# Delta rule: four state updates on VectorE moved from the end of a round to its middle

## What is computed

```
def step(S, inp):
    q_i, k_i, u_i, w_i, g_i, a_i = inp
    v_new = u_i - w_i @ S
    o = (q_i * exp(g_i)) @ S + a_i @ v_new
    S = S * exp(g_last) + k_dec.T @ v_new        # the state update
    return S, o
...
o = rmsnorm(o, gdn_norm_g) * silu(gate)          # needs the sum of o's squares
```

## Time and profile before

| | |
|---|---|
| median of 3 runs | 2711.78 us (2711.27 to 2712.54) |
| the profiled execution | 2711.7 us, span 2709.9 us |
| mean granted TensorE clock | 0.991 |
| busy: TensorE, weight loads, VectorE, ScalarE, GpSimd | 2604.8, 2173.4, 1664.5, 843.2, 1131.1 us |
| rounds 1 to 7 of the delta rule | roughly from 360 to 590 us |
| of 340 to 576 us: TensorE, VectorE, ScalarE, GpSimd busy | 213.64, 170.38, 73.28, 14.79 us |

### The profile page before, as it was taken

How to read it: one execution, slowest core, us unless ns; L and a number is a source line. 1 busy time by engine, 2 the same in 40 slices (tenths; PEclk the granted TensorE clock), 3 DMA queues, 4 the chain that set the end, 5 groups by cost and what they waited for, 6 DMA issues and landing times.

```text
span 2709.9 us, 33153 instructions
## 1 busy us (share of the span) xinstructions
PE 2604.8 (96%) x13218; PEld 2173.4 (80%) x13218; DVE 1664.5 (61%) x2192; ACT 843.2 (31%) x1332; POOL 1131.1 (42%) x651
## 2 busy tenths in 40 slices
PE   6999889989999999999999998999999999999998
PEld 5788778877788877888888887788888888888877
DVE  4879968766412587666674558804455465476566
ACT  4011233334223433333332436312222222243342
POOL 2433100046732546777754444663222322242364
PEclk8999999999999999999999999999999999999999
DMA  4122233235311412222245553472433342466682
GB/s 151 63 87 94 97 122 126 90 105 203 117 55 70 160 68 78 78 86 78 86 143 192 168 174 133 170 253 105 132 101 109 132 141 93 159 253 210 218 310 109
DMA packets 147381, 360.25 MB, mean 133 GB/s; under 512 B 15173, under 2 KB 51229, under 8 KB 147100
## 3 DMA queue, kind: packets, MB, share of 16 engines
q1 hardware_dynamic: 65072, 177.81, 19.6%
q10 hardware_dynamic: 82156, 180.33, 18.6%
HBM read 268.90 MB, written 89.19 MB: 132 GB/s over the span
## 4 chain that ended last, share of the span: by engine, by line
PE 84%; DVE 7%; ACT 2%; DMA 2%; POOL 2%; issue 2%; ACTq 1%; DVEq 0%; POOLq 0%
PE pp L295 31%; PE pp L2177 13%; PE pp L2230 9%; PE pp L277 8%; PE pp L493 7%; PE pp L2907 2%; PE pp L1254 2%; DMA w_raw<-in_weights 1%; POOL w_lo L3606 1%; DVE hgin_b L2713 1%; PE pp L1941 1%; PE pp L1920 1%; DVE hgin_f L2703 1%; POOL w_hi L3604 1%; PE pp L2927 1%
## 5 line engine op out<-in xcount | busy, mean ns | idle before, releaser
L3604 POOL CAST w_hi<-w_raw 128x1024 fp32r<-128x1024 f32 x184 | 222.6, 1210 | 1010.2 <-PE pp L295 678.2
L295 PE MATMUL pp<-w_hi,act_hi 128*128 128x512 f32 x1344 | 540.9, 402 | 14.1 <-POOL w_lo L3606 8.8
L295 PE MATMUL pp<-w_hi,act_lo 128*128 128x512 f32 x1344 | 527.9, 393 | 0.0
L295 PE MATMUL pp<-w_lo,act_hi 128*128 128x512 f32 x1344 | 525.2, 391 | 0.0
L3606 POOL TENSOR_TENSOR w_lo<-w_raw,w_hi 128x1024 fp32r<-128x1024 f32 x184 | 467.6, 2541 | 14.7
L295 PEld LDWEIGHTS pp<-w_hi,act_hi 128*128 128x128 f32 x1344 | 253.4, 189 | 69.6 <-POOL w_lo L3606 9.5
L295 PEld LDWEIGHTS pp<-w_hi,act_lo 128*128 128x128 f32 x1344 | 252.9, 188 | 58.1
L295 PEld LDWEIGHTS pp<-w_lo,act_hi 128*128 128x128 f32 x1344 | 253.7, 189 | 51.3
L493 PE MATMUL pp<-act_hi,w_hi 128*128 128x512 f32 x480 | 191.1, 398 | 15.2 <-DVE act_lo L834 6.5
L2148 POOL TENSOR_TENSOR w_lo<-w_raw,w_hi 128x1024 fp32r<-128x1024 f32 x52 | 134.2, 2582 | 164.3 <-ACT w_hi L2142 164.3
L493 PE MATMUL pp<-act_lo,w_hi 128*128 128x512 f32 x480 | 188.7, 393 | 0.0
(11 more groups left out here) (467 smaller groups left out, 5293.1 us busy)
## 6 DMA issues: line engine op xcount, KB each, us to landing
w_raw<-in_weights SPq DMA_DIRECT2D x314, 512.0 KB, 3.5
z_s<-hg_st ACTq DMA_DIRECT2D x52, 512.0 KB, 3.9
hid_s<-ffn_cb ACTq DMA_DIRECT2D x22, 512.0 KB, 2.6
ffn_graw<-hid_s ACTq DMA_DIRECT2D x44, 256.0 KB, 3.1
hg_qkb<-hT_s SPq DMA_DIRECT2D x16, 512.0 KB, 8.2
qkvT_s<-mixin_o ACTq DMA_DIRECT2D x12, 512.0 KB, 2.8
gdn_qkv<-qkvT_s ACTq DMA_DIRECT2D x8, 768.0 KB, 6.2
front_x<-in_x ACTq DMA_DIRECT2D x8, 512.0 KB, 5.1
```

The lines of the kernel that those rows point to most:

```text
L295: last = pe.matmul(dst, a[:, k, t * P:(t + 1) * P], columns(w, j, k, 0, n), start=(k == 0 and a is high and w is w_hi), stop=(k == NK - 1 ...
L3604: pool.tensor_copy(hi, raw).then_inc(w_split, 1)
```

## The change

The four state updates stand in the middle of the round, ahead of `oss`, in place of its end behind `u6`. The list of steps is put in the same order. `oT` waited for `s3` and now waits for `og`, since the bank O1 is free by then. In the last state round (tile 7), which has no update, its four steps are counted with `gg` in place of `og`. No instruction is added or taken away on any engine.

```diff
-self.ov = Steps(sem("gdn_o_dve"), "gg oss om " + recip_sqrt_steps("on") + " oy on og s0 s1 s2 s3 lo", 0)
+self.ov = Steps(sem("gdn_o_dve"), "gg s0 s1 s2 s3 oss om " + recip_sqrt_steps("on") + " oy on og lo", 0)
...
                     if 0 <= o - 1 < NT:
-                        after(pe, self.ov, "s3" if o < NT else "og", o - 1)
+                        after(pe, self.ov, "og", o - 1)
...
-OV.done(tt(self.gate[o % 2][:, :, :], self.gate[o % 2][:, :, :], row(self.gn[:, :]), ALU.mult), "gg")
+OV.done(tt(self.gate[o % 2][:, :, :], self.gate[o % 2][:, :, :], row(self.gn[:, :]), ALU.mult), "gg", *(("s0", "s1", "s2", "s3") if o == NT - 1 else ()))
...
                     long(2)
+                    if state and o < NT - 1:
+                        after(dve, self.os, "ds", o)
+                        for h in range(GH):
+                            OV.done(stt(self.S[:, h, :], self.S[:, h, :], sm[:, 5, o, h:h + 1], b4(self.O1)[:, h, :], ALU.mult, ALU.add), f"s{h}")
                     if state:
                         after(dve, self.oa, "osq", o)
                         OV.done(dve.tensor_reduce(s4[:, 4, :], self.osq[:, :, :], AX_X, ALU.add), "oss")
...
-                        skipped = ("s0", "s1", "s2", "s3") if o == NT - 1 else ()
-                        OV.done(tt(self.on[:, :, :], self.on[:, :, :], self.gate[o % 2][:, :, :], ALU.mult), "og", *skipped)
+                        OV.done(tt(self.on[:, :, :], self.on[:, :, :], self.gate[o % 2][:, :, :], ALU.mult), "og")
                     if inv:
                         update(i, 6)
-                    if state and o < NT - 1:
-                        after(dve, self.os, "ds", o)
-                        for h in range(GH):
-                            OV.done(stt(self.S[:, h, :], self.S[:, h, :], sm[:, 5, o, h:h + 1], b4(self.O1)[:, h, :], ALU.mult, ALU.add), f"s{h}")
                     long(CT * CTAPS)
```

## The result

The changed kernel takes 2719.54 us in the median (12 runs, 2714.2 to 2721.4), the kernel before, timed beside it, 2711.53 us (12 runs, 2705.57 to 2716.62). The ratio is 1.0028, with a 95% interval of 1.0019 to 1.0037: 7.6 us slower, between 5.2 and 10.0. The forecast was 2715.5 us, the range ended at 2718.5, and the likeliest class was "within 0.2%": the direction was right, the size was not.

A forecast was written before the change was run, and what follows sets the result against it. TensorE was taken as the bound, with two chains releasing `oT` in turn. Terms 0.67 + 1.04 + 2.06 - 0.32 + 0.65 - 0.32 + 0 = 3.78 us on 2711.7 gave 2715.5 us, range 2711.0 to 2718.5.

The forecast's parts named there:

- Its mechanism: Rounds' second halves: `u6` leaving `oT`'s way gains 0.32 us; `u5` and `y(6)` come 1.04 us later, 2.06 in odd rounds.
- rival C: TensorE idling 2 us more in rounds 3 and 5 may drop its clock: 5.5 us in all, 2717.2 us; chance 0.10.
- C's other half: Shorter idle time in round 6 may remove the clock drop there: 2713.8 us; chance 0.05.
- the cover in round 1: The second `ada`'s 1.39 us wait for weights hides part of the 2.06 us delay, leaving 0.67 lost.
- the pass-on: Behind the stage TensorE runs with hardly a gap, so the 3.8 us reach the whole time in full.
- The expected 1.4 us of `c6`: Rounds 1, 3 and 5: GpSimd's sum holds VectorE's `c6`, the L1750 product behind `on_m`, making it 1.4 us long.
- Rival A: Odd rounds: `c6` isn't held, it or `om` precedes GpSimd; `y(6)` 1.04 us late, not 2.06; 2712.8 us; chance 0.15.
- Rival B: Rounds 1, 3, 5: GpSimd's second sum also goes first, `c6` waits 0.81 us more; 2717.9 us; chance 0.15.
- Rival D: VectorE takes the updates in a mid-round wait of its own; gain 3 to 5 us, 2707 to 2709; chance 0.08.
- The class: Whole kernel: within 0.2% (5.4 us) 0.74, slower by more 0.23, faster by more 0.03.

The follow-up runs named there:

- the second trace of the kernel before: Kernel before, unedited, traced again: 2708.92 us against 2711.16, ratio 0.9997; 206.66 us from `qe0` of round 1 to `oT` behind round 7.
- fill4: Changed kernel plus four needless TensorE products in the idle time ahead of `y(6)` in rounds 1, 3 and 5: 2715.99 us, ratio 1.0016 to the kernel before.
- pool_later: Changed kernel with GpSimd's first sum of odd rounds (L1231) waiting for `og`: 2715.05 us, ratio 1.0011 to the kernel before.
- the second measurement: Changed kernel measured once more, no edit: 2718.05 us against 2711.4 for the kernel before, ratio 1.0023.
- swap: Kernel before with only the order of `u6` and the four updates turned round at the round's end: 2709.14 us, ratio 0.9991.
- late: Changed kernel with the updates moved behind `u5`, the copies and `x1`, still ahead of `og`: 2707.7 us, ratio 0.9989 to the kernel before.
- best: Updates behind `x1`, GpSimd's first odd-round sum behind `og`, needless products at three idle places: 2706.07 us against 2709.25 for the kernel before, ratio 0.9984.
- fill: Changed kernel plus eight needless TensorE products ahead of `y(6)` in rounds 1, 3 and 5: 2719.75 us, ratio 1.0029 to the kernel before.

## Why the prediction was wrong, point by point

**Its mechanism held, but for the clock.** `u5` is late by 1.04 us, by 2.08 in the odd rounds; `u6` is out of `oT`'s way for 0.32 to 0.34; the updates are not stretched; the wait for `ds` costs nothing; nothing behind `oT` is touched. `oT` is released by the step that I named in every round. Only the way to it is another in rounds 1 and 3: `ss` doesn't wait for `sq` any more (no idle time ahead of 468.04), since TensorE comes to it late by its own slow products. Term by term, against the second trace of the kernel before:

| round | predicted | changed kernel | of it the clock (changed less fill4) | the rest |
|---|---|---|---|---|
| 1 | +0.67 | +3.67 | 1.55 | +2.12 |
| 2 | +1.04 | +1.01 | 0.00 | +1.01 |
| 3 | +2.06 | +3.68 | 1.58 | +2.10 |
| 4 | -0.32 | -0.34 | -0.01 | -0.33 |
| 5 | +0.65 | +1.64 | 1.08 | +0.56 |
| 6 | -0.32 | -0.34 | 0.00 | -0.34 |
| sum | +3.78 | +9.32 | 4.20 | +5.12 |

The rest splits once more by pool_later: 80.28 - 78.40 = 1.9 us come from the place of the updates alone, 83.52 - 80.28 = 3.2 from GpSimd's hold. The split is rough in round 5, where pool_later also frees `x6`.

**The step that failed: the clock.** I saw that a fall behind 3.13 us of idle time costs 1.7 us, wrote that the change adds 2 us of idle time in rounds 3 and 5 (round 1 has it too), and then left it out of the sum, as rival C with a chance of 0.10 and the price of one fall. The sum gave TensorE's lateness and treated the time behind it as unchanged. In fact each of the three idle times brought a fall, in both executions, and they cost 1.55, 1.58 and 1.08 us, 4.2 together. Nor did the clock behind round 6 come back, as C's other half had it: `oT` waits 1.77 us there in place of 3.13 and still takes 0.98 us in place of its plain 0.66 (TensorE in the changed kernel):

```profile
566.34 0.98 PE L1584 MATMUL pp<-ident,gdn_on 128*128 128x128 f32 x4 [1.77 <-DVE gdn_on L1885]
```

**The second step that failed: the cover in round 1.** The term 2.06 - 1.39 = 0.67 took a wait for weights as a property of the kernel. It was of one execution. Without it the term is 2.06 (measured 2.12), and the sum without the clock would be 5.17 (measured 5.12). Against the first trace itself, which has that wait, the six halves are 87.72 - 79.99 = 7.7 us longer. The whole time changed by 7.6 us, and its interval, 5.2 to 10.0, holds 7.7 and 9.3 alike; the second measurement's, 3.5 to 8.9, holds only 7.7.

**Not shown: the pass-on.** I passed the stage's 3.8 us on to the whole in full. The time behind the stage differs by 5.5 us between two executions of the kernel before, so no run can confirm or refute that at this size.

**Right for a wrong reason: who is held.** The expected 1.4 us of `c6` did not come; `c6` took 0.41. `on_m` was held, from 459.46 to 460.68, and `c6` stood behind it. Since all of it is one queue, `u5` is late by the same amount (2.08 against the predicted 2.06). The Trainium skill's page "SBUF — State Buffer", section "Who interferes with whom", has VectorE and GpSimd blocking one another fully where the VectorE instruction works in a two-port mode within SBUF, a tensor-scalar one included; I had set that sentence aside, since no row showed it for four elements. The trace now agrees with it: 1.22 us in place of 0.17, and 1.22 to 1.24 in all six odd rounds of the two executions. In which mode `on_m` ran no trace shows.

**Rival A** did not happen, though half of its condition did: `c6` wasn't held, but `on_m` ahead of it was. Its working is what pool_later shows: -0.54 us in round 5, where A had about -0.3, and 1.04 in round 3. **Rival B** took a held `on_m` as the case in which GpSimd's second sum gets ahead of `c6`: the first half came, the second didn't. `c6` began at 460.59, ahead of the sum of L1233 (460.73). B's time, 2717.9 us, is the nearest to the result, by a mechanism that wasn't there. **Rival D** had no idle time on VectorE to stand on, and no row shows any. The gain that can be had is that of swap, late and best, by other means.

**The class.** The bound of 0.2% was 5.4 us; 3.8 us lay under it, 7.6 over. A clock term of one fall (1.7) would have brought the sum to 5.5, three would have brought it to 8.9.

## What to carry to other kernels

Of a step that is moved forward, ask what it delays on its own queue, and follow that to what ends the stage: here 1.04 us of VectorE work ahead of `u5` cost more than the 0.32 us that `u6` gave. Where a shift makes an instruction meet another engine's access to SBUF, cost the hold for every instruction in the window, small ones too; and where it makes TensorE idle longer, read in the rows how the granted clock went behind idle times of that length at such a place, and put it into the sum once for each place. A wait of about 1 us for a transfer in one execution is no cover to subtract: look at a second execution first.

## What the hardware showed beyond what was expected

- An idle time of 1.02 us ahead of `y(6)` (rounds 2 and 4 of the changed kernel, rounds 1, 3 and 5 of pool_later) left the granted clock behind it at 1.00; 2.08 us at the same place brought it to 0.50 six times of six. The length of one idle time doesn't tell by itself: 1.77 us ahead of `oT` behind round 6 of the changed kernel went with a fall, 1.74 us ahead of `oT` behind round 7 of best with none, and the fall in round 4 of best came 2 us behind an idle time of 0.96 us.
- 1.7 us of needless products in the 2.08 us kept the clock at 1.00 and paid for themselves with 1.1 to 1.6 us a round. A needless product costs 0.43 us in this form, and once it is longer than the idle time it costs that.
- A VectorE instruction on 128x4 elements, which takes 0.17 us, took 1.22 to 1.27 when it started less than 0.1 us behind the start of a sum on GpSimd (twelve times of twelve, in both executions of the changed kernel, fill and fill4); the sum itself kept its time, 1.26 to 1.29 us (1.30 before). GpSimd's next sum started while `c6` was at work (460.73, with `c6` from 460.59) and took 0.86 us in place of 0.73; `c6` kept its 0.41.
